# Six gate tiles per layer computed as three pairs of seven quarter products inside the attention loops of two mixer layers

## What is computed

```python
for l in range(DEPTH):                                        # DEPTH = 2
    shift, scale, gate = split(silu(c) @ w_ada[l] + b_ada[l], 3)
    hx = rms_norm(x, norm_g[l]) * (1 + scale) + shift         # hc likewise from ctx
    px = split_cols(hx @ w_in[l])       # q, k, v, g_att(512), c_a, c_b, g_conv(256), f_u, g_four(256)
    attn = windowed_attention(rope(q), rope(k), v, kc, vc, attn_sink[l])
    y = concat([attn * silu(g_att), conv(c_a, c_b) * silu(g_conv), fourier(f_u) * silu(g_four)]) @ w_out[l]
    if l == 0: ctx = ctx + gate_c * yc                        # context stream: first layer only
    x = x + gate * y
return second_block(rms_norm(x, final_g), mem, ...)
```

## Time and profile before

| | us |
|---|---|
| median of three runs | 1026.39 |
| range of the three | 1026.29 to 1027.01 |
| own time of the profiled execution | 1026.29 |
| its span | 1024.5 |
| first layer's attention, 145.7 to 244.8 | PE busy 97.64 of 99.10; DVE 51.28, ACT 45.20, POOL 15.38 |
| second layer's projections, 299.4 to 360.2 | PE busy 60.80 of 60.80; DVE 39.12, ACT 23.72, POOL 0.00 |
| second layer's attention up to the values, 360.2 to 388.5 | PE busy 28.30 of 28.30; DVE 16.10, ACT 12.89, POOL 1.49 |

### The profile page before, as it was taken

The page is one execution under the profiler, slowest core; times in us unless marked ns, Lnnn a source line. Parts: engine busy times, 40 slices in busy tenths (PEclk is TensorE's granted clock), DMA queues, the critical chain, the costliest instruction groups (busy, mean ns, idle before and its releaser), DMA issues.

```text
span 1024.5 us, 15340 instructions
## 1 busy us (share of the span) xinstructions
PE 1000.3 (98%) x5676; PEld 710.9 (69%) x5676; DVE 512.5 (50%) x1398; ACT 354.5 (35%) x861; POOL 85.9 (8%) x140
## 2 busy tenths in 40 slices
PE   6999999999999999999999999999999999999996
PEld 2458554556887777988999877899999744444442
DVE  5459836447365667566865824853534510000004
ACT  5224133435043247245475134742121411111113
POOL 0061000032200004300000000000000010000000
PEclk9999999999999999999999999999999999999999
DMA  9972124762233422364354352058647799999996
GB/s 362 420 303 95 42 82 178 291 272 83 83 123 130 158 83 70 130 236 139 115 202 163 126 202 83 2 195 328 237 186 307 295 396 420 419 422 420 421 419 248
DMA packets 34518, 227.57 MB, mean 222 GB/s; under 512 B 4641, under 2 KB 4913, under 8 KB 9200
## 3 DMA queue, kind: packets, MB, share of 16 engines
q1 hardware_dynamic: 31360, 214.97, 53.4%
q10 hardware_dynamic: 1920, 9.80, 2.5%
q0 software_dynamic: 1168, 1.85, 0.5%
HBM read 222.15 MB, written 8.41 MB: 225 GB/s over the span
## 4 chain that ended last, share of the span: by engine, by line
PE 90%; DVE 6%; DMA 2%; ACT 1%; issue 1%; SPq 0%; DVEq 0%; ACTq 0%
PE lin L669 12%; PE sc L686 11%; PE lin L1398 11%; PE sc L792 6%; PE aux L1398 5%; PE lin L686 4%; PE aux L1246 4%; PE sc L892 4%; PE lin L856 3%; PE sc L1363 3%; PE sc L669 3%; PE aux L922 3%; PE sc L1071 3%; PE lin L908 2%; DVE UN L2284 2%; DMA Y<-ada_in 2%
## 5 line engine op out<-in xcount | busy, mean ns | idle before, releaser
L669 PE MATMUL lin<-H,ring 128*128 128x256 f32 (+1 forms) x560 | 125.8, 385 | 0.0
L669 PEld LDWEIGHTS lin<-H,ring 128*128 128x128 f32 x560 | 106.0, 190 | 18.0 <-issue 4.2
L792 PE MATMUL sc<-H,ring 128*128 128x512 f32 (+1 forms) x192 | 67.3, 496 | 0.0
L1614 ACT ACTIVATE SP<-lin 128x512 f32<-128x512 f32 (+2 forms) x88 | 42.0, 485 | 72.7 <-PE lin L908 72.6
L2284 DVE SCALAR_TENSOR_TENSOR UN<-UN,cols 128x512 f32<-128x512 f32 (+1 forms) x120 | 66.7, 627 | 0.0
L2196 DVE CUSTOM_DVE_ANT_0 SP<-sc,CW,SK 128x512 f32<-128x512 f32 (+1 forms) x48 | 31.8, 662 | 53.6 <-PE sc L892 53.6
L1625 ACT ACTIVATE SP<-SP,ST 128x513 f32<-128x513 f32 (+4 forms) x88 | 53.8, 611 | 6.7 <-DVE ST L2199 6.4
L792 PEld LDWEIGHTS sc<-H,ring 128*128 128x128 f32 x192 | 34.8, 189 | 30.3 <-issue 25.6
L2851 DVE TENSOR_TENSOR PR<-lin,PR 128x512 f32<-128x512 f32 x8 | 5.5, 692 | 94.5 <-PE lin L1398 94.5
L892 PE MATMUL sc<-PR 64*128 64x256 f32 (+3 forms) x240 | 42.2, 434 | 2.3 <-DVE ST L2196 1.5
L1246 PE MATMUL aux<-Y,ring 128*128 128x256 f32 x192 | 42.0, 379 | 0.2 <-DVE PR L2645 0.2
(11 more groups left out here) (503 smaller groups left out, 1867.6 us busy)
## 6 DMA issues: line engine op xcount, KB each, us to landing
ring<-w_stream SPq DMA_DIRECT2D x119, 1024.0 KB, 6.7
SP<-w_stream SPq DMA_DIRECT2D x14, 1024.0 KB, 20.3
UN<-w_stream SPq DMA_DIRECT2D x10, 1024.0 KB, 18.2
PR<-w_stream SPq DMA_DIRECT2D x8, 1024.0 KB, 17.0
CW<-w_stream SPq DMA_DIRECT2D x8, 1024.0 KB, 16.4
X<-w_stream SPq DMA_DIRECT2D x8, 1024.0 KB, 18.7
Y<-w_stream SPq DMA_DIRECT2D x8, 1024.0 KB, 18.2
PR<-ada_in SPq DMA_DIRECT2D x5, 1024.0 KB, 26.4
```

The lines of the kernel that those rows point to most:

```text
L669: m = mm(dst, w[:, k, :], rhs(k), start=n == 0, stop=n == KT - 1)
L792: m = mm(bank[:, 0:ns * SEQ], filling["w"][:, k, :], H[:, 0:ns, k, :], start=k == 0, stop=k == KT - 1)
L1614: fn(PT[:, g % TURNED, a:b], take()[:, 0:b - a], ACT.Copy).then_inc(lin_taken, 1)
```

## The change

The six gate tiles of each layer become three pairs of seven quarter products. In the first layer a step of `fill` does one quarter (four matmuls with 256 columns), 21 steps in place of 24. In the second a step does a piece of two quarters (four matmuls each with 128 columns) and the last piece of a pair one quarter. The quarters go into two half banks in turn, each of which DVE must have read first (`quarter_added`), and DVE joins them into `P1` where ACT copied. POOL makes the sums of weight quarters for all six pairs, copies three of the sums of token quarters that `paired_in` used (first layer), and makes four new ones (second layer). A modulation chunk is summed in two halves: ACT copies the first, DVE adds the second. Chunk 2 is turned between the two halves of the first `paired_out`, and `memory_again` moves from step 32 to the first gate multiplication of the tail. The sums of weight quarters for the first layer's `paired_out` go into other buffers, `unit_free` of a pair's unit comes after its seventh quarter.

```diff
+FILLS = ([("ada", x, half) for x in (1, 2) for half in range(2)], [])
+GATE_PAIRS = GATES // 2
+SEQUENCE = (("ada", 1, 0, 2), ("gate", 0, 0, 7), ("ada", 1, 2, 2), ("gate", 1, 0, 7), ("ada", 2, 0, 2), ("gate", 2, 0, 7), ("ada", 2, 2, 2))
...
-          [("gate", t, 4 * q) for t in range(GATES) for q in range(2)])
-FILL_STEPS = ([*PIECES[0][:30], None, *PIECES[0][30:]],
+FILL_STEPS = ([*PIECES[0][:11], None, *PIECES[0][11:14], None, *PIECES[0][14:25], None, *PIECES[0][25:27], None, *PIECES[0][27:]],
               [*PIECES[1][:10], None, None, PIECES[1][10], None, None, None, PIECES[1][11]])
-ADA_TURNS = {13: 1, 25: 2}
...
+        def piece_bank(j, q):
+
+            return sc[:, j % 2, 512 + q % 2 * P:512 + (q % 2 + 1) * P]
+        def fill_bank(q):
+
+            return sc[:, q % 2, 512:512 + SEQ]
...
+            def gate_quarter(x, q):
...
+                if q == 0:
+                    pe.wait_ge(quarter_added, F_ADDED + n)
+                if q == 1:
+                    pe.wait_ge(fill_taken, ADA_BLOCKS + x + 1)
+                if q >= 2:
+                    pe.wait_ge(quarter_added, F_ADDED + n - 1)
+                if q == 0:
+                    m = quarter(fill_bank(q), w[:, 0, lo], H[:, 0, 0:4, :])
+                if q == 1:
+                    m = quarter(fill_bank(q), w[:, 0, hi], H[:, 0, 4:8, :])
+                if q == 2:
+                    pe.wait_ge(weights_mixed, 4 * (F_MIX + x) + 1)
+                    m = quarter(fill_bank(q), s1, t1)
+                if q == 3:
+                    pe.wait_ge(weights_mixed, 4 * (F_MIX + x) + 3)
+                    m = quarter(fill_bank(q), s2, t2)
...
+                if q == 6:
+                    m = quarter(fill_bank(q), w[:, 1, hi], t4)
+                    at["owed"] += 1
+                m.then_inc(quarter_made, 1)
+            def gate_piece(x, qs):
...
+                if j >= 2:
+                    pe.wait_ge(quarter_added, G1_ADDED + sum(len(f[2]) for f in PIECES[1][:j - 1]))
...
+                    if q == 2:
+                        pe.wait_ge(weights_mixed, 4 * (G1_MIX + x) + 3)
+                        pe.wait_ge(tokens_mixed, G1_TOKENS + 3)
+                        m = quarter(dst, s1, t1)
+                    if q == 3:
+                        m = quarter(dst, s2, t2)
...
+                    m.then_inc(quarter_made, 1)
+
             def fill(layer, i):
-                ns = 2 - layer
-                if i < len(FILL_STEPS[layer]) and FILL_STEPS[layer][i]:
...
-                        if k0 == 0:
-                            filling["w"] = block_of_weights()
-                        for k in range(k0, k0 + PER_STEP[layer]):
-                            m = mm(bank[:, 0:ns * SEQ], filling["w"][:, k, :], H[:, 0:ns, k, :],
-                                   start=k == 0, stop=k == KT - 1)
...
+                step = FILL_STEPS[layer][i] if i < len(FILL_STEPS[layer]) else None
+                if layer == 0 and step and step[0] == "gate":
+                    gate_quarter(*step[1:])
+                elif step and step[0] == "gate":
+                    gate_piece(*step[1:])
...
+                    if k0 % 4 == 0:
+                        pe.wait_ge(fill_taken, n)
...
+                        else:
+                            pe.wait_ge(quarter_added, F_ADDED + 7 * (n - ADA_BLOCKS) - 1)
+                    m = ada_step(bank, k0)
+                    if k0 % 4 == 2:
                         m.then_inc(fill_ready, 1)
...
-                    else:
-                        ns = 2 - layer
-                        fn(P1[:, GA + x, 0:ns, :], bank[:, 0:ns * SEQ], ACT.Copy).then_inc(fill_taken, 1)
+                step = FILL_STEPS[layer][i] if i < len(FILL_STEPS[layer]) else None
+                if layer == 0 and step and step[::2] == ("ada", 2):
+                    act.wait_ge(fill_ready, fill_of(step[1], 0) + 1)
+                    fn(SQ[:, step[1] - 1, :], sc[:, 1, 512:1024], ACT.Copy).then_inc(fill_taken, 1)
...
+            pool.wait_ge(tokens_mixed, F_TOKENS)
+            pool.wait_ge(quarter_added, 1)
+            nc.gpsimd.tensor_copy(T_FILL[0], T_IN[0]).then_inc(tokens_mixed, 1)
+            nc.gpsimd.tensor_copy(T_FILL[3], T_IN[3]).then_inc(tokens_mixed, 1)
+            pool.wait_ge(quarter_made, F_PART)
+            pool.wait_ge(four_ready, 2)
+            mixed(F_MIX, FILL_UNIT[0], *LO_HI, S_FILL)
+            pool.wait_ge(lin_ready, turn["l0", GF + 1] + 1)
+            pool.wait_ge(tokens_mixed, F_TOKENS + 2)
+            nc.gpsimd.tensor_copy(T_FILL[1], T_IN[1]).then_inc(tokens_mixed, 1)
             pool.wait_ge(sinks_ready, 1)
+            mixed_before = {14: 1, 24: 2}
             for name in ("l0", "l1"):
+                if name == "l1":
+                    h11, h12, h21, h22 = (H[:, 0, k:k + 4, a:a + P] for k in (0, 4) for a in (0, P))
+                    g1, g3, g2, g4 = T_GATE
+                    pool.wait_ge(shifted["l1"], KT)
+                    nc.gpsimd.tensor_tensor(g1, h12, h11, ALU.subtract).then_inc(tokens_mixed, 1)
+                    nc.gpsimd.tensor_tensor(g3, h22, h12, ALU.subtract).then_inc(tokens_mixed, 1)
+                    pool.wait_ge(tokens_mixed, G1_TOKENS + 1)
+                    nc.gpsimd.tensor_tensor(g2, h22, g1, ALU.subtract).then_inc(tokens_mixed, 1)
+                    pool.wait_ge(tokens_mixed, G1_TOKENS + 3)
+                    nc.gpsimd.tensor_tensor(g4, h21, g2, ALU.subtract).then_inc(tokens_mixed, 1)
+                    pool.wait_ge(normed["l1"], 2 * KT)
+                    for x, to in enumerate((S_FILL, S_GATE)):
+                        mixed(G1_MIX + x, FIRST_OUT[1] - GATE_PAIRS + x, *LO_HI, to)
                 for i, it in enumerate(STAGES[name]):
                     g = first[name] + i
+                    if g in mixed_before:
+                        x = mixed_before[g]
+                        pool.wait_ge(quarter_made, F_PART + 7 * x - 1)
+                        mixed(F_MIX + x, FILL_UNIT[x], *LO_HI, S_FILL)
+                    if g == first["l1"] + 8:
+                        pool.wait_ge(quarter_made, G1_PART + 6)
+                        mixed(G1_MIX + 2, FIRST_OUT[1] - GATE_PAIRS + 2, *LO_HI, S_FILL)
                     if g >= HELD:
                         pool.wait_ge(probs_ready, g - HELD + 1)
                     nc.gpsimd.tensor_copy(S_of(g)[1][:, 0:1], SK[:, it["sink"]:it["sink"] + 1]).then_inc(sink_in, 1)
                 layer = int(name == "l1")
...
-                    mixed(len(PAIRED) + 4 * layer + n, FIRST_OUT[layer] + n, *LO_HI[::-1], S_OUT[4 * layer + n])
+                    mixed(OUT_MIX[layer] + 4 * layer + n, FIRST_OUT[layer] + n, *LO_HI[::-1], S_OUT[4 * layer + n])
...
+                def gate_quarter(x, q):
...
+                    if q == 0:
+                        v.tensor_copy(c12, bank).then_inc(quarter_added, 1)
+                        dve.wait_ge(quarter_added, added + 1)
+                        v.tensor_tensor(c11, c12, bank, ALU.add).then_inc(quarter_added, 1)
+                    if q == 2:
+                        v.tensor_copy(c22, bank).then_inc(quarter_added, 1)
+                    if q == 3:
+                        v.tensor_tensor(c12, c12, bank, ALU.add).then_inc(quarter_added, 1)
+                    if q == 4:
+                        dve.wait_ge(quarter_added, added + 4)
+                        v.tensor_tensor(c21, c12, bank, ALU.add).then_inc(quarter_added, 1)
+                        step(v.tensor_tensor(c12, c12, c22, ALU.add))
+                        dve.wait_ge(quarter_added, added + 5)
+                        joined_at[0] = step(v.tensor_tensor(c22, c22, c21, ALU.add))
+                    if q == 5:
+                        after(joined_at[0])
+                        v.tensor_tensor(c12, c12, bank, ALU.add).then_inc(quarter_added, 1)
+                    if q == 6:
+                        v.tensor_tensor(c21, c21, bank, ALU.add).then_inc(quarter_added, 1)
+
+                joined_at = [0]
+
                 def between(p):
+                    for i in (2 * p, 2 * p + 1):
+                        if layer == 0 and i < len(FILL_STEPS[0]) and FILL_STEPS[0][i] and FILL_STEPS[0][i][0] == "gate":
+                            gate_quarter(*FILL_STEPS[0][i][1:])
+                        if layer == 1 and i < len(FILL_STEPS[1]) and FILL_STEPS[1][i]:
+                            for q in FILL_STEPS[1][i][2]:
+                                gate_quarter(FILL_STEPS[1][i][1], q)
...
+                            x = FILL_STEPS[0][i][1]
+                            n, b = fill_of(x, 1), 1
+                            dve.wait_ge(fill_ready, n + 1)
+                            dve.wait_ge(fill_taken, n)
+                            v.tensor_tensor(SQ[:, x - 1, :], SQ[:, x - 1, :], sc[:, b, 512:1024], ALU.add).then_inc(fill_taken, 1)
...
+                    dve.wait_ge(tokens_mixed, F_TOKENS + 3)
...
                 for c in (0, 2):
+                    if c and layer == 0:
+                        modulation(2)
```

(3 more changed lines are left out.)

150 lines of the change are left out of this document (99 added, 51 removed).

## The result

The changed kernel takes 1041.95 us (median of four runs, 1039.72 to 1044.48) against 1026.58 us: ratio 1.0151, 95% interval 1.0138 to 1.0164. It is slower by 15.4 us; I had forecast 4.8 slower with an upper end at 1038.0. The profiled execution is the fastest of the four, 1039.72 us, span 1037.9, 13.4 us above the span before.

A forecast was written before the change was run, and what follows sets the result against it. PE's matmul queue was taken as the bound (98% busy, 90% of the chain). Gain 6.4 us against costs of 11.2 us gave +4.8 us on the profiled 1026.3, so 1031.1 us; range 1021.5 to 1038.0.

The forecast's parts named there:

- mix 1: Second layer, before the token tiles: POOL's weight mixing delays DVE's rotation and ACT's copy; cost 1.2 us, ends 0 and 2.0.
- the end of the attention: Second layer, 388.50 to 402.80: DVE nearly always busy, so added readings and additions are paid; 1.8 us, ends 0.3 and 3.3.
- the pieces: Second layer's attention: piece 4 waits for DVE's addition behind scalings, beside POOL's mix 2; 2.3 us, ends 0.4 and 4.2.
- the token sums: Second layer, near 301.7 us: four POOL sums beside DVE's shifts delay a bank; cost 2.3 us, ends 0 and 3.8.
- Gain in the first layer: PE in the first layer's attention: 24 steps removed, 21 quarters added, −5.2 us.
- step 9: First layer: modulation step waits for DVE's addition after the reciprocal while POOL may mix; 0.8 us, between 0 and 2.2.
- its tail: First layer's attention end: second `paired_out` unit mixed late, delaying DVE's multiplications and PE's products; 1.0 us, from −0.6 to 2.5.
- Rival C: Handshake in full: second-layer quarters wait for DVE, DVE for POOL; four terms 13.3 instead of 7.6, 1036.8 us; chance 0.08.
- the lock alone: Second layer's token sums: exclusive port lock costing DVE 1.27 us per POOL sum would make the term 3.6 us, not 2.3.
- its gain by count: PE in the second layer: 12 steps removed, 168 records of 128 columns added; −1.6 us, of which −1.2 counts.

The follow-up runs named there:

- nomix2: Changed kernel with POOL's four weight sums for the second layer's third gate pair left out; 1036.42 us.
- gate_first: Changed kernel with DVE adding the second layer's quarters ahead of the scalings of the pair before; 1035.09 us.
- moved4: Changed kernel with copies behind convolution, second-layer token sums and first two gate pairs' sums late, additions before scalings, two `paired_out` sums ahead of sinks 12, 14; 1026.67 us.
- l0_late: Changed kernel with the second layer's gates as before and the first layer's two copies behind the convolution's last tap; 1024.62 us, ratio 0.9985.
- all_moved: Changed kernel with copies behind convolution, token sums behind shifts, all three second-layer gate pairs' sums between rotations and attention, DVE's additions ahead of scalings; 1032.67 us.
- keepclock: Changed kernel with dummy matmuls ahead of three PE waits in the second layer's attention; 1038.89 us.
- late_sums: Changed kernel with second-layer token sums after stream 1's shifts and the first two gate pairs' weight sums after the last rotation; 1034.55 us.

## Why the prediction was wrong

The direction was right, and so was the kind of cause: POOL's work holds DVE up, and PE waits. Three sizes in the second layer were too small, and two terms were missing: the clock, and the third copy with the first mix of the first layer. The profiled execution is 13.4 us longer than before where I had 4.8. Of the 8.6 us between, 4.4 are clock, 1.7 the token tiles (below with mix 1), 0.9 the end of the attention, 0.8 the pieces, 0.5 the third copy and 0.4 the token sums; small differences both ways fill the rest.

- **Gain in the first layer**, with step 9 and its tail: forecast −5.2 + 0.8 + 1.0 = −3.4 us. Measured −4.0 in the attention and +0.8 behind it (0.4 a longer wait, 0.4 the turn of chunk 2, which moved there), −3.2 in all. Right in sum, though the split was off: no wait shows at step 9, for which I took 0.8, and the waits of the tail grew by 1.5, for which I took 1.0.
- **The third copy** and the first mix of the first layer, which no term of the sum covers: measured 0.5, most of it from the copy beside DVE's squares.
- **The token sums**: forecast 2.3, measured 2.7. Right within its ends; the loss per sum was 1.07 us, not 0.94, since POOL's sums took 1.33 to 1.45 us here: two shifts took 1.77 us for each sum, where they take 0.69 alone.
- **Mix 1** of the second layer: forecast 1.2 with an upper end of 2.0, measured 2.9. The other step that failed is that I looked at mix 1 alone and let its loss stop at ACT's gaps. Mix 0, which I did not cost, meets the rotation at 324 us, and DVE works through from there without a gap, so its 1.6 us are still there when mix 1 adds 4.0.
- **The pieces**: forecast 2.3, upper end 4.2, measured 3.1 of wait. I had both causes and took the middle of ends that are far apart, which no row supported. nomix2 and gate_first show that removing either cause leaves only 0.2 to 0.3 us.
- **The end of the attention**: forecast 1.8. Measured 2.7 us of waits above those of before (1.64 + 1.52 against 0.44). Two pairs of DVE's scalings stand beside the mixes as before (2.16 and 2.21 us, before 2.15 and 2.22), but four additions now stand ahead of the next reads and the last scalings, 2.6 us in all, and the two from SBUF take 0.77 and 1.36 of it. I had priced the waits of these two at 0.7; they came to 1.6.
- **The clock**, the step that failed by most: every wait was priced at its own length, and the matmuls behind it at full speed. The granted clock falls behind some of them and slows the matmuls that follow: 4.4 us in the profiled execution; the others, with a lower mean clock, took up to 4.8 us longer. Rows of before did not show it for waits of this kind: within the attentions PE waited at most 0.76 us at a time, and behind its 1.36 us at 31.25 the clock stayed at 1.00. They showed it only at the end of the program, where PE has stopped and the clock reads 0.50 from 1020 us.

Rival C (the second layer's terms at their upper ends, 1036.8) was the nearest, and also short for want of the clock: its four terms come to 13.3 us, the waits measured at these places to 11.4. The Trainium skill's lock (SBUF — State Buffer, "SBUF: two separate sides") concerns DVE operations with two SBUF inputs or in a two-port mode. The rows after agree on which operations are held up: an addition with one input in PSUM kept 0.28 us beside POOL, four with both in SBUF took 1.15, 0.28, 0.77 and 1.36. On the size, the 3.6 us that the lock alone gave for the token sums was further from the measured 2.7 than my 2.3.

The second layer in moved4 takes 108.9 us up to `paired_out` where it takes 107.3 in l0_late, 1.6 us more. Its waits there (0.77, 0.29, 1.11, 0.60, 0.35 and 0.60 us) are 3.3 us above the 0.44 of before, and its gain by count is 1.2 to 1.6, which fits. Another 0.5 us lies between the first `paired_out` and the second layer. What stays open is whether another placement of the sums would pay, and why the clock falls behind the same wait in some executions and not in others.

## What to carry to other kernels

A helper engine's "free" work had a price on another engine here: before moving sums to POOL, look at DVE's rows of the same microseconds, and count on it that a stream of operations with two SBUF inputs, or of scalings in SBUF, loses about 1 us for each POOL sum of 128x512 beside it (0.94 and 1.07 us in these rows). Carry delays through the whole unbroken stream of that engine, not to the next gap in another one. Where TensorE carries the chain, a wait of a few microseconds can cost more than itself (4.80 us of wait became 7.8 in all_moved), and a spread of the executions with a lower mean clock was its sign.

## What the runs showed of the hardware

- The clock fell to its lower level (0.50 granted, 1.2 of 2.4 GHz) behind waits of PE in stretches that were otherwise fully busy: in the changed kernel for some 4 us behind 3.10 us at 378, and for some 6 us behind 1.64 and 1.52 us in close succession at 411 to 413. It did not do so each time: behind the wait of 2.7 us near 308 us it fell in keepclock (0.86 from 310 to 320) and not in the changed kernel's profiled execution, and behind the tail's waits of 1.66 and 1.53 us it did not fall in late_sums.
- A few dummy matmuls in such waits closed the scatter of the runs: 4.8 to 0.5 us, and 3.5 to 0.7 us.
- Beside POOL, a DVE scaling of 128x512 went from 0.44 to 1.45 us, while additions and reads with one PSUM input kept their time. POOL loses as well: its copy of 128x1024 took 1.04 us alone (l0_late) and 1.42 and 1.50 us beside DVE's taps.
